# Two-block transformer stack on one core: stage borders slice by slice, joint high products and a joint last pair of down units in the FFNs

## The reference

```python
def rmsnorm_2(x, g, eps=NORM_EPS):
    xf = x.astype(jnp.float32)
    y = xf * lax.rsqrt(jnp.mean(xf * xf, -1, keepdims=True) + eps)
    return (y * g.astype(jnp.float32)).astype(x.dtype)

def swiglu(x, w_gate, w_up, w_down):
    return (jax.nn.silu(x @ w_gate) * (x @ w_up)) @ w_down
...
        hdn = swiglu(rmsnorm_2(x, ng[0]), ffn1_w_gate[layer], ffn1_w_up[layer], ffn1_w_down[layer])
        x = x + 0.5 * rmsnorm_2(hdn, ng[1])
        hdn = rmsnorm_2(x, ng[2])
...
        x = x + rmsnorm_2(hdn, ng[3])
        hdn = swiglu(rmsnorm_2(x, ng[4]), ffn2_w_gate[layer], ffn2_w_up[layer], ffn2_w_down[layer])
        x = x + 0.5 * rmsnorm_2(hdn, ng[5])
```

## Time and profile before

| | |
|---|---|
| median of 3 runs | 2077.37 us (2075.97 to 2081.43) |
| profiled execution | 2076.58 us, span 2074.7 us |
| mean granted PE clock | 0.913 |
| PE busy | 1868.9 us, 90% |
| DVE busy | 992.9 us, 48% |
| ACT busy | 588.9 us, 28% |
| POOL busy | 35.7 us, 2% |
| read from HBM | 402 MB, 194 GB/s over the span |

### The profile page before, as it was taken

How to read it: one execution, slowest core, us unless ns; L and a number is a source line. 1 busy time by engine, 2 the same in 40 slices (tenths; PEclk the granted TensorE clock), 3 DMA queues, 4 the chain that set the end, 5 groups by cost and what they waited for, 6 DMA issues and landing times. The chain is left out here.

```text
span 2074.7 us, 33276 instructions
## 1 busy us (share of the span) xinstructions
PE 1868.9 (90%) x14452; PEld 1475.6 (71%) x14452; DVE 992.9 (48%) x1893; ACT 588.9 (28%) x871; POOL 35.7 (2%) x18
## 2 busy tenths in 40 slices
PE   6999999889998699979996899989997988759998
PEld 5544456675443499968885799979996776548997
DVE  4122243251211466642278565556665654556664
ACT  2000012231000343321134443343333402125332
POOL 0000000000000100000000010000000000101000
PEclk9688999788998899999997899999999989779999
DMA  9799970357999655513420355535542312034540
GB/s 367 285 418 425 424 283 28 127 223 312 424 426 425 279 183 183 184 36 142 166 98 1 122 187 190 190 119 188 183 163 94 130 51 84 4 142 163 185 161 21
DMA packets 58155, 405.49 MB, mean 195 GB/s; under 512 B 6368, under 2 KB 7776, under 8 KB 10384
## 3 DMA queue, kind: packets, MB, share of 16 engines
q1 hardware_dynamic: 58000, 403.25, 50.6%
HBM read 402.17 MB, written 1.05 MB: 194 GB/s over the span
## 5 line engine op out<-in xcount | busy, mean ns | idle before, releaser
L1787 PE MATMUL ps<-ffn_xh,ffn_wh 128*128 128x256 f32 x1408 | 404.8, 287 | 28.5 <-DVE ffn_xl L1902 28.5
L1788 PE MATMUL ps<-ffn_xl,ffn_wh 128*128 128x256 f32 x1408 | 403.5, 287 | 0.0
L1789 PE MATMUL ps<-ffn_xh,ffn_wl 128*128 128x256 f32 x1408 | 403.2, 286 | 0.0
L1878 DVE TENSOR_TENSOR ffn_wl<-w,ffn_wh 128x2048 fp32r<-128x2048 f32 (+1 forms) x136 | 304.3, 2238 | 15.9 <-ACT ffn_wh L1844 14.7
L1787 PEld LDWEIGHTS ps<-ffn_xh,ffn_wh 128*128 128x128 f32 x1408 | 275.5, 196 | 31.0 <-DVE ffn_wl L1878 29.5
L1788 PEld LDWEIGHTS ps<-ffn_xl,ffn_wh 128*128 128x128 f32 x1408 | 275.5, 196 | 1.6
L1789 PEld LDWEIGHTS ps<-ffn_xh,ffn_wl 128*128 128x128 f32 x1408 | 275.4, 196 | 0.0
L1844 ACT CAST ffn_wh<-w 128x2048 fp32r<-128x2048 f32 (+1 forms) x136 | 247.1, 1842 | 18.4 <-PEq L2299 8.2
L1858 ACT ACTIVATE ffn_sil<-ffn_zg 128x256 f32<-128x256 f32 x88 | 36.8, 418 | 418.6 <-DVE ffn_zg L1885 418.6
L1885 DVE TENSOR_TENSOR ffn_zg<-ps,rs 128x256 f32<-128x256 f32 x88 | 37.4, 425 | 246.7 <-PE ps L1789 246.5
L1787 PE MATMUL ps<-ffn_wh,ffn_hidh 128*128 128x512 f32 x352 | 137.4, 390 | 0.0
(11 more groups left out here) (503 smaller groups left out, 2825.7 us busy)
## 6 DMA issues: line engine op xcount, KB each, us to landing
w<-in_ffn_gu SPq DMA_DIRECT2D x88, 1024.0 KB, 4.9
w<-in_moe_gu SPq DMA_DIRECT2D x78, 1024.0 KB, 15.7
w_extra<-in_moe_gu SPq DMA_DIRECT2D x50, 1024.0 KB, 17.8
w<-in_ffn_dn SPq DMA_DIRECT2D x44, 1024.0 KB, 4.9
w_extra<-in_moe_dn SPq DMA_DIRECT2D x32, 1024.0 KB, 17.0
w<-in_moe_dn SPq DMA_DIRECT2D x32, 1024.0 KB, 17.6
w<-in_ab_xbc SPq DMA_DIRECT2D x6, 1024.0 KB, 4.8
w<-in_ab_out SPq DMA_DIRECT2D x6, 1024.0 KB, 4.9
```

What stands on the lines that cost most here:

```text
L1787: nc.tensor.matmul(out, wh, xh, start=start, stop=False)
L1788: nc.tensor.matmul(out, wh, xl, start=False, stop=False)
L1789: return nc.tensor.matmul(out, wl, xh, start=False, stop=stop)
L1878: nc.vector.tensor_tensor(low[:, s, at], S.buf(units[n])[:, at], high[:, s, at], ALU.subtract).then_inc(*w_split.one())
```

## The change

- **FF_ORDER**: the last two gate/up units move ahead of dn 8, so that dn 8, 9 and 10 are last.
- **Joint high products**: `ffn_xh` and `ffn_xl` become the two halves of one tensor `ffn_x`. High weights meet both in one matmul of 512 columns, remainders of the weights meet the high half in one of 256. Gate and up take a bank each, high by remainder lies in the upper 256 columns. ACT copies these to `ffn_part_low`, DVE adds them to the lower ones and scales gate and up in one go. Two pairs of banks alternate.
- **Start of an FFN**: PE takes unit 0 as high products of slices 0 to 3, then 4 to 7, then the low ones. POOL makes the two half remainders of unit 0. DVE makes remainders 1 and 2 ahead of the first scaling. The ones matmul comes behind unit 1. Squares are taken slice by slice.
- **Last two down units** run by token half: dn 9 and dn 10 for t = 0, then both for t = 1. PSUM banks of gate/up and down change sides from stage to stage (`rows_at`, `free_at`).
- **Borders**: the second half's transposes and the updates of `h` move from the post norm's block into the next stage's, slice by slice, interleaved with rounding (`AfterPost`), with the pre norm (`NormAfterPost`) or with the store in four transfers. `rms_norm` and `final_norm` are gone; ahead of ffn1_0 `AfterExperts` makes the final norm slice by slice into `xn`, and POOL copies it to `h` later. RWKV's shift is made slice by slice between the mixes.

```diff
-    FF_ORDER += [("dn", _u)] + [("gu", b) for b in (2 * _u + 4, 2 * _u + 5) if b < FF_T]
+    FF_ORDER += [("dn", _u)] + [("gu", b) for b in (2 * _u + 4, 2 * _u + 5) if b < FF_T - 2]
+FF_ORDER[-3:-3] = [("gu", FF_T - 2), ("gu", FF_T - 1)]
...
-            sp.dma_start(out, K.h[:, :, 0:SEQ]).then_inc(*saved.dma())
+            for k in range(0, KT, 2):
+                sp.wait_ge(*post.updated.at(k + 2))
+                sp.dma_start(out[:, k:k + 2], K.h[:, k:k + 2, 0:SEQ]).then_inc(*saved.dma())
...
+    def update(self, dve, k):
+        nc, K = self.K.nc, self.K
+        dve.wait_ge(*self.turned.at(k // 2 + 1))
+        nc.vector.scalar_tensor_tensor(out=K.h[:, k, 0:SEQ], in0=self.turned_tile(k), scalar=self.gain[:, k:k + 1],
+                                       in1=K.h[:, k, 0:SEQ], op0=ALU.mult, op1=ALU.add).then_inc(*self.updated.one())
...
+    def scalar(self, act):
+        K, nc = self.K, self.K.nc
+        for k in range(KT):
+            act.wait_ge(*self.post.updated.at(k + 1))
+            nc.scalar.activation(self.X[:, k], K.h[:, k, 0:SEQ], ACT.Square).then_inc(*self.squared.one())
+        act.wait_ge(*self.summed.at(1))
+        nc.scalar.activation(K.rs[:, 0, 0:SEQ], self.total(), ACT.Sqrt, bias=K.eps[:, 0:1], scale=1.0 / D).then_inc(*self.rooted.one())
+    def root(self, dve):
+        K, nc = self.K, self.K.nc
+        for k in range(KT):
+            self.post.update(dve, k)
+        dve.wait_ge(*self.post.updated.at(KT))
+        dve.wait_ge(*self.rooted.at(1))
+        link(dve, self.inverse, nc.vector.reciprocal(K.rs[:, 1, 0:SEQ], K.rs[:, 0, 0:SEQ]))
...
+            def by_high(b, s, a, k):
+                return nc.tensor.matmul(pair_of(b)[:, a], high[:, s, tile(a, k)], X[:, k], start=k == 0, stop=False)
+            def by_low(b, s, a, k):
+                return nc.tensor.matmul(pair_of(b)[:, a, 0:SEQ], low[:, s, tile(a, k)], XH[:, k], start=False, stop=k == KT - 1)
+            def gate_up_first():
+                for k0 in range(0, KT, 4):
+                    for a in range(2):
+                        pe.wait_ge(*w_high.at(a + 1))
+                        for k in range(k0, k0 + 4):
+                            pe.wait_ge(*x_split.at(k + 1))
+                            by_high(0, 0, a, k)
+                for a in range(2):
+                    pe.wait_ge(*first_split.at(a + 1))
+                    for k in range(KT):
+                        mm = by_low(0, 0, a, k)
+                return mm
             def gate_up(b, n):
-                if b >= 4:
-                    pe.wait_ge(*up_scaled.at(b - 3))
-                s = n % parts
+                if b >= 2:
+                    pe.wait_ge(*added.at(b - 1))
+                pe.wait_ge(*w_split.at(n))
                 for a in range(2):
-                    pe.wait_ge(*w_split.at(a + 1 if n == 0 else n + 2))
                     for k in range(KT):
-                        if n == 0 and a == 0:
-                            pe.wait_ge(*x_split.at(k + 1))
-                        w = slice((a * KT + k) * P, (a * KT + k + 1) * P)
-                        mm = split_matmul(K.ps[:, b % 4, a * SEQ:(a + 1) * SEQ], high[:, s, w], low[:, s, w], XH[:, k], XL[:, k],
-                                          k == 0, k == KT - 1)
+                        by_high(b, n % parts, a, k)
+                        mm = by_low(b, n % parts, a, k)
                 return mm
...
-            for n, (what, i) in enumerate(FF_ORDER):
+            entry.tensor(pe)
+            for n, (what, i) in enumerate(FF_ORDER[0:last]):
                 if what == "gu":
-                    gate_up(i, n).then_inc(*unit_done.one())
-                    if n == 0:
+                    (gate_up(i, n) if n else gate_up_first()).then_inc(*unit_done.one())
+                    if n == 1:
                         pe.wait_ge(*summed.at(3))
-                        nc.tensor.matmul(K.ps[:, 7, 0:SEQ], K.con(C_ONE), sq[:, 0], start=True, stop=True).then_inc(*totalled.one())
+                        nc.tensor.matmul(total, K.con(C_ONE), sq[:, 0], start=True, stop=True).then_inc(*totalled.one())
                     continue
-                pe.wait_ge(*w_split.at(n + 2))
+                pe.wait_ge(*w_split.at(n))
                 pe.wait_ge(*hid_made.at(2 * i + 2))
                 if i == 0:
                     pe.wait_ge(*rooted.at(1))
+                if n < last - 1:
+                    for t in range(2):
+                        mm = down(i, n % parts, t)
+                    mm.then_inc(*unit_done.one())
+                    continue
                 for t in range(2):
-                    mm = down(i, n % parts, t)
-                    if n == last:
-                        mm.then_inc(*post.made.one())
-                if n < last:
-                    mm.then_inc(*unit_done.one())
-            pe.wait_ge(*up_scaled.at(FF_T))
-            post.tensor(pe)
+                    down(i, n % parts, t)
+                    if t == 0:
+                        pe.wait_ge(*w_split.at(last))
+                        pe.wait_ge(*hid_made.at(2 * i + 4))
+                    down(i + 1, last % parts, t).then_inc(*post.made.one())
+            pe.wait_ge(*added.at(FF_T))
+            post.turn(pe, 0)
...
+            def round_tokens(k):
+                act.wait_ge(*entry.ready(k))
+                nc.scalar.activation(XH[:, k], entry.src(k), ACT.Copy, scale=g_in[:, k:k + 1]).then_inc(*x_high.one())
+            entry.scalar(act)
             round_unit(0, 0)
             for k in range(KT):
-                nc.scalar.activation(XH[:, k], K.h[:, k, 0:SEQ], ACT.Copy, scale=g_in[:, k:k + 1]).then_inc(*x_high.one())
-            round_unit(0, 1)
+                round_tokens(k)
+                if k in (1, 3, 5):
+                    round_unit(k // 3, (1, 0, 1)[k // 2])
             for j in range(2):
-                nc.scalar.activation(sq[:, 4 * j:4 * j + 4], K.h[:, 4 * j:4 * j + 4, 0:SEQ], ACT.Square).then_inc(*squared.one())
-            round_unit(1)
-            act.wait_ge(*totalled.at(1))
-            nc.scalar.activation(K.rs[:, 0, 0:SEQ], K.ps[:, 7, 0:SEQ], ACT.Sqrt, bias=K.eps[:, 0:1], scale=1.0 / D).then_inc(*rooted.one())
+                for k in range(4 * j, 4 * j + 4):
+                    last_square = nc.scalar.activation(sq[:, k], entry.src(k), ACT.Square)
+                last_square.then_inc(*squared.one())
             round_unit(2)
             for n, (what, i) in enumerate(FF_ORDER):
                 if what == "gu":
-                    act.wait_ge(*gate_scaled.at(i + 1))
-                    nc.scalar.activation(sil[:, i % 2], zg[:, i % 2], ACT.Silu).then_inc(*silu_made.one())
+                    act.wait_ge(*unit_done.at(n + 1))
+                    if i:
+                        act.wait_ge(*added.at(i))
+                    nc.scalar.copy(part_low[:], pair_of(i)[:, :, SEQ:]).then_inc(*low_copied.one())
                 if n + 3 <= last:
                     round_unit(n + 3)
+                if what == "gu":
+                    if i == 0:
+                        act.wait_ge(*totalled.at(1))
+                        nc.scalar.activation(K.rs[:, 0, 0:SEQ], total, ACT.Sqrt, bias=K.eps[:, 0:1], scale=1.0 / D).then_inc(*rooted.one())
+                    act.wait_ge(*scaled.at(i + 1))
+                    nc.scalar.activation(sil[:, i % 2], z[:, i % 2, 0], ACT.Silu).then_inc(*silu_made.one())
+            entry.settled(act)
             post.scalar(act)
...
+            for part in range(2):
+                pool.wait_ge(*w_high.at(part + 1))
+                at = slice(part * half_unit, (part + 1) * half_unit)
+                nc.gpsimd.tensor_tensor(low[:, 0, at], S.buf(units[0])[:, at], high[:, 0, at], ALU.subtract).then_inc(*first_split.one())
...
+            def remainder(n):
+                dve.wait_ge(*w_high.at(n + 3))
                 s = n % parts
-                nc.vector.tensor_tensor(low[:, s, at], S.buf(units[n])[:, at], high[:, s, at], ALU.subtract).then_inc(*w_split.one())
+                nc.vector.tensor_tensor(low[:, s], S.buf(units[n]), high[:, s], ALU.subtract).then_inc(*w_split.one())
             def scale(b):
+                dve.wait_ge(*low_copied.at(b + 1))
+                nc.vector.tensor_tensor(z[:, b % 2], pair_of(b)[:, :, 0:SEQ], part_low[:], ALU.add).then_inc(*added.one())
                 if b == 0:
                     dve.wait_ge(*rooted.at(1))
                     link(dve, K.dve_step, nc.vector.reciprocal(rs, K.rs[:, 0, 0:SEQ]))
-                dve.wait_ge(*unit_done.at(order["gu", b] + 1))
-                nc.vector.tensor_tensor(zg[:, b % 2], K.ps[:, b % 4, 0:SEQ], rs, ALU.mult).then_inc(*gate_scaled.one())
-                nc.vector.tensor_tensor(zu[:, b % 2], K.ps[:, b % 4, SEQ:2 * SEQ], rs, ALU.mult).then_inc(*up_scaled.one())
+                dve.wait_ge(*added.at(b + 1))
```

(16 more changed lines are left out.)

279 lines of the change are left out of this document (174 added, 105 removed).

## The result

The changed kernel takes 2055.1 us, the median of executions between 2050.3 and 2060.0; the kernel before takes 2079.4 beside it. The ratio is 0.988, interval 0.985 to 0.990. It is faster, but by 24 us where 46 were forecast, and outside the range of 2017 to 2046.

A forecast was written before the change was run, and what follows sets the result against it. PE bounds the FFNs inside; at borders it waits for ACT and DVE chains. Gains of 15.0, 13.8, 6.4, 6.0, 3.6 and 3.1 make 47.9, less 2 for the clock: from 2076.6 to 2031 us, range 2017 to 2046.

The forecast's parts named there:

- Joint high products: Gate/up units of the FFNs: a 512 and a 256 replace three 256s, 0.013 us saved each time, 15.0 us in all.
- Rival 1: Gate/up units: the joint product saves nothing, the surplus goes with columns or weight loads; 2046 us, chance 0.08.
- What pays for it: Gate/up units: the added ACT copy (0.59 us) and DVE add and scaling (0.70 each) stay hidden behind PE.
- rival 4: Gate/up units: DVE becomes the bound at scale, remainder and products; slower, 2127 us, chance 0.03.
- A border behind a post norm: Starts of ffn2_0, ffn1_1 and ffn2_1: first down unit at T + 34.2, T the previous stage's last matmul end; gains 13.8 us.
- rival 3: FFN starts: POOL and DVE delay each other, slow stretches follow waits, 2 to 3 us per FFN; 2041 us, chance 0.17.
- Then a new wait: Each FFN's start: PE stands 3.1 us in front of unit 3 for its remainder; 2 us given back for the clock.
- Into ffn1_0: Border into ffn1_0: first matmul 8.6 us after the block's start instead of 15.75, first down unit at 38.0; gains 6.4 us.
- Into NSA: Border into NSA: first matmul at T + 12.0 instead of 18.0 later; gains 6.0 us (5 to 8).
- RWKV: RWKV's start: reciprocal ends at T + 11.4 instead of 15.4, slices to the first mix cost 0.9; gains 3.6 us.
- Rival 2: FFN starts: no wait in front of unit 3, since steps set in series overlap; 2016 us, chance 0.10.
- Rival 5: Borders stay as long because ACT's casts are last in each start; only 18.3 us come, 2058 us, chance 0.03.

The follow-up runs named there:

- e7: e5 with POOL idle in an FFN's start: DVE makes the two half remainders of unit 0 and the three sums of squares; 2025.1 us, 0.974 of before.
- e11: The changed kernel itself, unaltered, measured and traced a second time; 2055.1 us, 0.989 of before.
- e5: Changed kernel with unit 3's remainder made before the wait for the root, and low products behind the eight high ones; 2044.7 us, 0.984 of before.
- e6: e5 with PE kept busy by transposes of a constant in its idle time at FFN borders; 2041.4 us, 0.982 of before.
- e9: e7 with PE kept busy by transposes of a constant in its idle time at FFN borders; 2019.5 us, 0.972 of before.
- e1: Changed kernel with unit 0's two half remainders made by DVE, leaving POOL only its three sums; 2062.2 us, 0.992 of before.
- e3: Changed kernel with each joint high product of 512 columns split into two matmuls of 256 again; 2068.4 us, 0.995 of before.

## Why the prediction was wrong, step by step

- **Joint high products**, 15.0: 6.9. The step that failed is that a 512 and a 256 in turn cost what each costs among its own kind: the pair took 0.353 us, not 0.346. Rival 1 named the doubt; the truth lies half way. In the other orders the pair takes 0.348, and the bodies give 13.1 to 14.1.
- **What pays for it**: right, 0.59 and 0.69 us, and DVE never the bound of a steady unit (rival 4 falls).
- **A border behind a post norm**, 13.8: -3.6. The layout was right as far as it can be compared: with POOL idle it is met to 0.1 us at the last token remainder. Behind that it is untested, since DVE then carries POOL's work too: the first down unit of e7 comes at T + 33.5 where the layout without the wait gives 31.1. The failed step is "POOL's two half remainders ... end by 9 at the latest, when PE has just finished the high products". They did end by then, in ffn2_0 at T + 8.7 or t = 5.9, and nobody waited for them. The step put them at no cost to DVE, whose token remainders stood in the sum at 0.5 us each; beside POOL two of them took 2.1 to 2.3. This is rival 3, at twice its price: on average 5.8 us per FFN, with ffn1_0, against 2 to 3 there. Of these 23.4 us, by the trace, 13.3 are DVE instructions of the four starts held by POOL (12.1 in token remainders, 1.2 in the norm's product) and 8.4 the slow unit 3; this adds delays as if each moved the border by itself.
- **Then a new wait**: right to 0.2 us in all four FFNs (2.87 or 2.88 where 3.1 was forecast), but its aftermath, 1.4 to 2.8 us of slow clock each and 8.4 in all, was given 2 for all.
- **Into ffn1_0**, 6.4: 0.4, by the same two causes.
- **Into NSA**, 6.0: 8.3. The first product comes at T + 11.1, 0.9 ahead of the forecast, and the next 8 us ran at a clock of 1.00 where before they had 0.80:

```profile
923.37:931.37 8.00, 8.00 (x30) 6.80 (x31) 0.42 (x1) 0.00 (x0) 0.00 (x0) 0.80 0.00 0
```

```profile
914.81:922.81 8.00, 8.00 (x37) 7.07 (x38) 3.48 (x9) 0.00 (x0) 0.00 (x0) 1.00 0.01 2
```

  The first is before, the second after. In e11 the start was later, T + 12.8, and NSA took 269.4; why it was later is open.
- **RWKV**, 3.6: 1.9. PE's 200th product with a weight unit starts 4.3 us earlier behind T than before, so the step held, though the prediction put the old reciprocal's end at T + 15.4 here too and it was T + 15.9. The block then ran longer at 1.2 GHz (89 us of it, 79 before), which differs from trace to trace of the same code, 72 to 99. In e11 it was 72, and RWKV took 268.4, a gain of 5.0.
- **The end**, 3.1: 3.0. First joint down units: into ffn1_1 the border with POOL idle is as short as the others (33.6 against 33.5), where before it was 2.4 longer.
- Rival 2 (no wait) falls. Rival 5 (borders as long, 2058 us) was near in its time and in the borders, but not in its cause: the slices do run early, and an FFN's first product came 2.7 to 6.0 us sooner than before.

## What to carry to other kernels

When work goes to an engine that is free, ask which engine shares a path with it, and put it there only while the other has instructions that don't need that path; here taking two small jobs from POOL shortened the four borders by 12.9 us, where the whole change gave 24. Look for the sign in the trace that you have: here an instruction of DVE already took longer beside POOL than elsewhere before the change. A new wait on PE costs its own length and often a slow clock behind it, but a slow clock costs nothing where PE waits for others anyway. A pace read among instructions of one form is not the pace of the mixture; look for one place in the trace where the forms stand in turn.

## What the hardware showed that I had not expected

- POOL and DVE took turns by whole instructions when both had two SBUF inputs: a DVE instruction of 0.47 us took up to 2.43, one of 2.28 up to 4.49; with one operand in PSUM it kept its 0.47.
- A 512 and a 256 in strict alternation took 0.353 us a pair, in twos or eights 0.348, against 0.346 from their own paces.
- PE at 1.2 GHz for 10.2 us of an FFN's start or for 3.4 (e5, e6), for 6.8 or for none (e7, e9): the same border to 0.1 us.
- In six traces the four waits of 2.8 to 3.0 us in front of unit 3 were followed by a loss of 1.3 to 2.8 us at 1.2 GHz, 22 times of 24; in ffn2_1 of e1 and of e3 by none.
